# The low parts of down's coefficients on GpSimd instead of VectorE, between its gathers

## The chip, the cores and the metric

The kernel runs on one core of one Trainium2 chip. The metric is the device time of one launch in microseconds (us), the median of several runs. Three runs of the kernel before took 1741.0, 1741.33 and 1743.81 us, so the median is 1741.33 us. The data are those of one decoder layer: 256 tokens, 2048 channels, 16384 experts.

## What is computed

One layer with a convolution part, a gated short convolution and, behind them, a mixture of rank-one experts ("PEER"). What matters here is the last step of the experts:

```python
def peer_block(x_tok, w_q, sub_keys, peer_u, peer_v):
    ...
    act = jax.nn.gelu(jnp.einsum('td,thkd->thk', x_tok, u_sel), approximate=False)
    coef = act * g.astype(act.dtype)
    v_sel = peer_v[experts]
    return jnp.einsum('thk,thkd->td', coef, v_sel)
```

Each token chooses 8 x 16 = 128 of the 16384 experts. The kernel computes the activations of all experts for all tokens (stage "up") and multiplies all of them, zero where an expert wasn't chosen, with all rows of peer_v (stage "down"). An exception: for the second half of the tokens (block 1) and the first half of the output columns, each token's 128 chosen rows are gathered and added one by one.

## The kernel before

**Split products.** A product in full fp32 is made of three products in the fast format fp32r: an operand is split into a high part (a copy by ScalarE, rounded to fp32r) and a low part (the original less the high part). TensorE multiplies high by high, high by low and low by high. For each unit of weights of 128 x 1024 fp32, the stream is: SyncE's queue loads it into a buffer (`raw` or `raw_late`, 7 of them in down), ScalarE makes `w_hi` (L643, in `hi`), VectorE makes `w_lo` (L863, in `lo`), TensorE uses both. There are four pairs `w_hi`, `w_lo`, so ScalarE may be at most three units ahead of TensorE (`HLEAD`, `LEAD`). A buffer `raw` is reloaded when the low part has been made.

**Down.** 256 units, in 32 groups of four tiles of hidden activations. A group's coefficients, 128 x 1024 fp32, are a slice of `hid`. ScalarE copies it to `c_hi` (L796, `coef_hi`), VectorE subtracts to make `c_lo` (L1323, `coef_lo`). Both parts are the stationary operands of TensorE's matmuls (L1640 to L1642, 512 columns each); the even groups up to 27 hold one unit that goes unsplit in fp32 (L1651, 4 matmul records). Groups 0 to 27 use two sets `c0` and `c1` in turns (`coef_slot`). ScalarE makes `c_hi` of group g + 1 when TensorE has begun group g (the table `coef_at`), and VectorE makes `c_lo` of it at the same place of its own list, so that it is ready almost a group ahead. Each group of 8 units has 72 matmuls (fewer with an unsplit unit): units of 6, 6, 12, 12, 6, 6, 12 and 12, as each of the four column chunks is made for one or two blocks of tokens (`ORDER`, `blocks_of`). TensorE's `group` waits for the count `clo_done` before a group's first matmul.

**The picks.** For the gathered part, GpSimd's queue issues two kinds of indirect DMAs, one pair after the other (`gather_rows`, L597: 128 rows of 4 KB, one per token; `gather_acts`, L603: 128 single coefficients). VectorE adds row k times its coefficient to an accumulator in PSUM (`pick`, L1342, 128 of them). There are four row buffers (three `rows`, and `row_late`), so row k is gathered when pick k - 4 is done (`picked_done`). The numbers of the units at which VectorE makes each pick are fixed (`pick_unit`), one in 1.77 units. `acts_issued` lets the first eight turns issue two coefficient gathers per row gather and the later ones one; there are none behind row 115. Gathered coefficients are used in eights, a good way behind.

**The order** on each engine is written out by hand, and each engine works through its own list in order. VectorE's loop over the units of down, in words: the low part three units ahead, the coefficients' low part if one is due here, the picks that are due here, the next unit. GpSimd's list in down is a row gather with its coefficient gather(s), again and again.

## Time and profile before

| | us |
|---|---|
| median of 3 runs | 1741.33 |
| the profiled execution, its time | 1742.71 |
| the profiled execution, its span | 1740.7 |
| TensorE busy | 1703.1 (98%) |
| VectorE busy | 1459.6 (84%) |
| ScalarE busy | 849.1 (49%) |
| GpSimd busy | 530.5 (30%) |

The span is what the trace covers; the run's own time has 2.0 us around it. TensorE's granted clock was 1.00 (its upper level, 2.4 GHz) from end to end but for the first and last few us. Down begins near 1180 us and ends near 1726 us. A row of the timeline gives start, duration and, in brackets, how long the engine had been idle and what ended that; "issue" is time in which it waited for nothing that the profile shows. PEld is TensorE's weight load. The busy time of matmuls is modelled, and their rows overlap.

### The profile page before, as it was taken

Reading aid. Unit: us, or ns where it says so; the run is one execution under the profiler, and the core shown is the slowest. Engines: PE = TensorE matmul, PEld = TensorE weight load, DVE = VectorE, ACT = ScalarE, POOL = GpSimd, SP = SyncE. Lnnn points to the kernel's source line nnn. Section 1 sums busy time; section 2 is a strip of 40 time slices with the busy share of each in tenths; the row PEclk is TensorE's granted clock in tenths of the full one; section 3 lists DMA queues with packets and bytes.
Section 4 is the critical chain, followed back from the end, with each engine's and each line's share of the span. In section 5 each row is a group of like instructions: output and inputs, shape, how many; then the busy total and the mean of one; then the engine's idle time right before and its main releaser. Section 6 shows DMA issues by size and latency. Waiting matters only on the chain.

```text
span 1740.7 us, 27889 instructions
## 1 busy us (share of the span) xinstructions
PE 1703.1 (98%) x10124; PEld 1495.6 (86%) x10124; DVE 1459.6 (84%) x2095; ACT 849.1 (49%) x1071; POOL 530.5 (30%) x342
## 2 busy tenths in 40 slices
PE   9999999899999999999999999999999999999997
PEld 9999987799999888888888888887777777777876
DVE  7999997678968788888888888666898889899997
ACT  5544436344544444544444444445455554555544
POOL 0000000287881000000000000004786767687731
PEclk9999999999999999999999999999999999999999
DMA  7787787777777777777777777898999999999994
GB/s 278 261 276 260 238 254 254 282 237 233 248 254 247 241 240 243 245 237 242 237 242 238 239 242 246 285 355 310 344 390 396 398 399 394 397 372 399 401 407 141
DMA packets 173757, 504.73 MB, mean 290 GB/s; under 512 B 19424, under 2 KB 35936, under 8 KB 172640
## 3 DMA queue, kind: packets, MB, share of 16 engines
q1 hardware_dynamic: 134000, 427.08, 71.0%
q0 software_dynamic: 22528, 67.19, 10.1%
q10 hardware_dynamic: 17136, 9.35, 1.8%
q8 instruction: 41, 0.67, 0.2%
q14 instruction: 52, 0.43, 0.1%
HBM read 490.98 MB, written 79.69 MB: 328 GB/s over the span
## 4 chain that ended last, share of the span: by engine, by line
PE 81%; DMA 6%; DVE 5%; issue 4%; POOL 2%; ACT 1%; DVEq 0%; SPq 0%; POOLq 0%; ACTq 0%
PE psum L1461 22%; PE psum L1462 12%; PE psum L1446 8%; PE psum L1444 8%; PE psum L1445 8%; PE psum L1640 5%; PE psum L1642 5%; PE psum L1641 5%; DMA raw<-in_v_w_dram 4%; DVE w_lo L863 2%; PE psum L1606 2%; POOL sp_coef L603 2%; PE psum L1464 1%; DMA rows<-v_rows,sp_idx 1%; PE psum L1510 1%
## 5 line engine op out<-in xcount | busy, mean ns | idle before, releaser
L643 ACT ACTIVATE w_hi<-raw 128x1024 fp32r<-128x1024 f32 x540 | 571.6, 1060 | 645.9 <-PE psum L1464 180.7
L863 DVE TENSOR_TENSOR w_lo<-raw,w_hi 128x1024 fp32r<-128x1024 f32 x472 | 574.5, 1224 | 139.7 <-ACT w_hi L643 137.0
L1461 PE MATMUL psum<-xt,w_hi 128*128 128x512 f32 x1650 | 583.1, 393 | 0.1
L1462 PE MATMUL psum<-xt,w_lo 128*128 128x256 f32 x1760 | 476.9, 281 | 0.0
L1461 PEld LDWEIGHTS psum<-xt,w_hi 128*128 128x128 f32 x1650 | 309.5, 188 | 63.2 <-issue 0.4
L597 POOL DMA_INDIRECT rows<-v_rows,sp_idx x96 | 135.1, 1407 | 720.7 <-issue 672.7
L1462 PEld LDWEIGHTS psum<-xt,w_lo 128*128 128x128 f32 x1760 | 331.9, 189 | 9.4
L1444 PE MATMUL psum<-xt,w_hi 128*128 128x256 f32 x1184 | 333.8, 282 | 3.1 <-issue 1.9
L1446 PE MATMUL psum<-xt,w_lo 128*128 128x256 f32 x1184 | 332.2, 281 | 0.0
L1445 PE MATMUL psum<-xt,w_hi 128*128 128x256 f32 x1184 | 330.5, 279 | 0.0
L1640 PE MATMUL psum<-w_hi,c_hi 128*128 128x512 f32 x726 | 290.1, 400 | 16.2 <-DVE w_lo L863 13.9
L1642 PE MATMUL psum<-w_hi,c_lo 128*128 128x512 f32 x726 | 282.8, 390 | 0.0
L1641 PE MATMUL psum<-w_lo,c_hi 128*128 128x512 f32 x726 | 282.8, 390 | 0.0
L586 POOL TENSOR_TENSOR w_lo<-raw,w_hi 128x1024 fp32r<-128x1024 f32 x68 | 164.6, 2427 | 363.4 <-ACT w_hi L643 363.3
L1444 PEld LDWEIGHTS psum<-xt,w_hi 128*128 128x128 f32 x1184 | 223.4, 189 | 3.6 <-issue 3.6
L1445 PEld LDWEIGHTS psum<-xt,w_hi 128*128 128x128 f32 x1184 | 223.5, 189 | 0.0
L1446 PEld LDWEIGHTS psum<-xt,w_lo 128*128 128x128 f32 x1184 | 223.1, 188 | 0.0
L603 POOL DMA_INDIRECT sp_coef<-hid_spill,sp_idx x128 | 176.8, 1381 | 53.9 <-issue 44.2
L1640 PEld LDWEIGHTS psum<-w_hi,c_hi 128*128 128x128 f32 x726 | 136.2, 188 | 57.6 <-DVE w_lo L863 23.9
L1641 PEld LDWEIGHTS psum<-w_lo,c_hi 128*128 128x128 f32 x726 | 136.3, 188 | 29.8 <-issue 2.6
L1642 PEld LDWEIGHTS psum<-w_hi,c_lo 128*128 128x128 f32 x726 | 136.3, 188 | 28.9
L643 ACT ACTIVATE w_hi<-raw_late 128x1024 fp32r<-128x1024 f32 x99 | 105.0, 1060 | 110.6 <-PE psum L1642 74.0
(175 smaller groups left out, 1695.2 us busy)
## 6 DMA issues: line engine op xcount, KB each, us to landing
raw<-in_u_w_dram SPq DMA_DIRECT2D x256, 512.0 KB
raw<-in_v_w_dram SPq DMA_DIRECT2D x148, 512.0 KB
v_rows<-in_v_w_dram SPq DMA_DIRECT2D x128, 512.0 KB, 5.2
raw_late<-in_v_w_dram SPq DMA_DIRECT2D x108, 512.0 KB
raw<-in_w_in_dram SPq DMA_DIRECT2D x80, 512.0 KB
raw<-in_w_out_dram SPq DMA_DIRECT2D x32, 512.0 KB
raw<-in_w_q_dram SPq DMA_DIRECT2D x32, 512.0 KB
hid_spill<-hid ACTq DMA_DIRECT2D x7, 1024.0 KB, 14.3
```

The costliest lines, as they stand in the source:

```text
L586: nc.gpsimd.tensor_tensor(w_lo[s][:, :], raw[:, s, :], w_hi[s][:, :].bitcast(f32), ALU.subtract).then_inc(lo_done[s], SPLIT)
L603: nc.gpsimd.indirect_dma_start(sp_coef[:, k:k + 1], None, hid_dram, bass.IndirectOffsetOnAxis(sp_idx[:, 0, k:k + 1], 0)).then_inc(act_in[k ...
L643: nc.scalar.activation(parts_of(slot_u)[0][:, :], raw_of(slot_u), ACT.Copy)\
L863: tt(lo_w[:, :], raw_of(slot_u), hi_w[:, :].bitcast(f32), ALU.subtract).then_inc(lo_done[slot_u % SPLIT], lo_step(u))
L1444: mm(dst, hi_w[:, sl], xt_hi[:, kk, :], start=st, stop=False)
L1445: mm(dst, hi_w[:, sl], xt_lo[:, kk, :], start=False, stop=False)
L1446: i = mm(dst, lo_w[:, sl], xt_hi[:, kk, :], start=False, stop=en)
L1461: mm(both, hi_w[:, sl], x_both, start=st, stop=False)
L1462: i = mm(both[:, 0:T], lo_w[:, sl], xt_hi[:, kk, :], start=False, stop=False)
L1640: mm(v_bank(j, b), c1, w1, start=st, stop=False)
L1641: mm(v_bank(j, b), c1, w2, start=False, stop=False)
L1642: i = mm(v_bank(j, b), c2, w1, start=False, stop=en)
```

## The change

GpSimd makes `c_lo` of groups 3 to 27 (`CLO_POOL = (3, G_LAST)`), 25 of 32, with the same operation on the same operands. VectorE keeps groups 0 to 2 and 28 to 31. The operation stands in GpSimd's list behind the row gather `gathered_before(g)` and its coefficient gather: that is the gather which waits for the last pick ahead of the place where VectorE made this `c_lo`. A new count, `clo_pool`, is raised by it; `wait_clo` makes each of those who waited for `clo_done` wait for the right one: TensorE at the start of each group, SyncE's queue at units 64 and 112 of down (for groups 4 and 8), ScalarE for groups 14 and 22.

```diff
+CLO_POOL = (3, G_LAST)
...
+def on_pool(g):
+
+    return CLO_POOL[0] <= g < CLO_POOL[1]
...
+def gathered_before(g):
+
+    at = U_DOWN + 2 * NCH * (g - 1) + 1
+    return len([k for k in range(PICKS) if pick_unit(k) < at]) + ROWS - 1
...
+        def wait_clo(engine, g):
+
+            a, b = CLO_POOL
+            if g >= a:
+                engine.wait_ge(clo_pool, min(g, b - 1) - a + 1)
+            if not on_pool(g):
+                engine.wait_ge(clo_done, g + 1 - (b - a if g >= b else 0))
...
+            def coef_lo_pool(g):
+                hi_c, lo_c = c_sets[coef_slot(g)]
+                pool.wait_ge(chi_done, g + 1)
+                nc.gpsimd.tensor_tensor(lo_c[:, :, :], hid[:, GROUP * g:GROUP * (g + 1), :],
+                                        hi_c[:, :, :].bitcast(f32), ALU.subtract).then_inc(clo_pool, 1)
...
             for k in range(ROWS, PICKS):
                 gather_rows(k)
                 gather_acts(acts_issued(k - 1), acts_issued(k))
+                for g in range(*CLO_POOL):
+                    if gathered_before(g) == k:
+                        coef_lo_pool(g)
...
             def coef_lo(g):
+                if on_pool(g):
+                    return
                 hi_c, lo_c = c_sets[coef_slot(g)]
...
             def group(g, slot, first=False):
-                pe.wait_ge(clo_done, g + 1)
+                wait_clo(pe, g)
```

Lines move by 21 to 32: the row gather is L618 in the changed kernel, the coefficient gather L624, the new operation L631, VectorE's `w_lo` L893, its `c_lo` L1355, a pick L1374, TensorE's three matmuls L1672 to L1674.

GpSimd's list where it reaches group 3 (`rows2` is gather 6, `row_late` gather 7, `rows0` gather 8). Before:

```order
L597 DMA rows2<-v_rows,sp_idx 128x1024 [waits picked_done]
L603 DMA sp_coef<-hid_spill,sp_idx 128x1 x2
L597 DMA row_late<-v_rows,sp_idx 128x1024 [waits picked_done]
L603 DMA sp_coef<-hid_spill,sp_idx 128x1 x2
L597 DMA rows0<-v_rows,sp_idx 128x1024 [waits picked_done]
```

Now:

```order
L618 DMA rows2<-v_rows,sp_idx 128x1024 [waits picked_done]
L624 DMA sp_coef<-hid_spill,sp_idx 128x1 x2
L631 TENSOR_TENSOR c1_lo<-hid,c1_hi 128x1024 [waits chi_done]
L618 DMA row_late<-v_rows,sp_idx 128x1024 [waits picked_done]
L624 DMA sp_coef<-hid_spill,sp_idx 128x1 x2
L618 DMA rows0<-v_rows,sp_idx 128x1024 [waits picked_done]
```

The low part of group 3 now stands between gather 6 with its two coefficient gathers and gather 7; every gather behind it is queued behind it and behind its wait for `c_hi`.

VectorE's list at the same group (the picks of rows 1 and 2 with the `w_lo` between them). Before:

```order
L1342 SCALAR_TENSOR_TENSOR psum<-rows1,sp_coef,psum 128x1024 [waits picked_done,rows_in1,coef_done]
L863 TENSOR_TENSOR w_lo2<-raw,w_hi2 128x1024 [waits hi_done]
L863 TENSOR_TENSOR w_lo3<-raw,w_hi3 128x1024 [waits hi_done]
L1323 TENSOR_TENSOR c1_lo<-hid,c1_hi 128x1024 [waits chi_done]
L1342 SCALAR_TENSOR_TENSOR psum<-rows2,sp_coef,psum 128x1024 [waits picked_done,rows_in2,coef_done]
```

Now:

```order
L1374 SCALAR_TENSOR_TENSOR psum<-rows1,sp_coef,psum 128x1024 [waits picked_done,rows_in1,coef_done]
L893 TENSOR_TENSOR w_lo2<-raw,w_hi2 128x1024 [waits hi_done]
L893 TENSOR_TENSOR w_lo3<-raw,w_hi3 128x1024 [waits hi_done]
L1374 SCALAR_TENSOR_TENSOR psum<-rows2,sp_coef,psum 128x1024 [waits picked_done,rows_in2,coef_done]
L893 TENSOR_TENSOR w_lo0<-raw,w_hi0 128x1024 [waits hi_done]
```

The pick of row 2 now follows the second `w_lo` directly, and with it everything behind moves up by one place.

## Rows read from the trace of the kernel before

**Rows 1.** the page, section 1: busy us (share of the span) by engine.
```profile
PE 1703.1 (98%) x10124; PEld 1495.6 (86%) x10124; DVE 1459.6 (84%) x2095; ACT 849.1 (49%) x1071; POOL 530.5 (30%) x342
```

**Rows 2.** windows of three stretches of down: busy us (x instructions) by engine, clock, DMA.
```profile
1210.00:1300.00 90.00, 84.47 (x356) 65.94 (x355) 76.97 (x69) 43.77 (x42) 70.95 (x55) 1.00 0.96 358
1300.00:1500.00 200.00, 193.59 (x820) 152.58 (x819) 174.97 (x156) 102.42 (x98) 139.84 (x105) 1.00 1.03 397
1500.00:1645.00 145.00, 142.20 (x607) 113.17 (x606) 136.49 (x122) 78.02 (x76) 115.50 (x78) 1.00 1.01 390
```

**Rows 3.** waits of PEld, 1210 to 1645: us in total, times, longest.
```profile
PEld psum L1640 <- DVE w_lo L863: 21.2, 20, 2.3
```

**Rows 4.** lines of VectorE, 1300 to 1500.
```profile
L863 DVE TENSOR_TENSOR w_lo<-raw,w_hi 128x1024 fp32r<-128x1024 f32 x49 | 59.5, 1226 | 2.7 <-ACT w_hi L643 2.6
L863 DVE TENSOR_TENSOR w_lo<-raw_late,w_hi 128x1024 fp32r<-128x1024 f32 x37 | 44.8, 1222 | 1.8 <-ACT w_hi L643 1.6
L1323 DVE TENSOR_TENSOR c_lo<-hid,c_hi 128x1024 fp32r<-128x1024 f32 x12 | 14.7, 1226 | 20.1 <-ACT c_hi L796 19.9 <-issue 0.3
```

**Rows 5.** one line, L1323, the low parts: ns min/median/max, first and last start.
```profile
L1323 DVE TENSOR_TENSOR c_lo<-hid,c_hi x32: 1217/1226/1229, 1159.5 to 1650.7; 128x1024 fp32r<-128x1024 f32 x32
```

**Rows 6.** lines of GpSimd, 1210 to 1300.
```profile
L603 POOL DMA_INDIRECT sp_coef<-hid_spill,sp_idx x30 | 36.0, 1200 | 10.4 <-issue 10.4
L597 POOL DMA_INDIRECT rows<-v_rows,sp_idx x19 | 26.8, 1411 | 7.0 <-issue 5.9 <-DVE psum L1342 1.1
L597 POOL DMA_INDIRECT row_late<-v_rows,sp_idx x6 | 8.5, 1416 | 1.8 <-issue 1.5 <-DVE psum L1342 0.3
```

**Rows 7.** lines of GpSimd, 1300 to 1500.
```profile
L603 POOL DMA_INDIRECT sp_coef<-hid_spill,sp_idx x53 | 68.9, 1300 | 16.1 <-issue 16.1
L597 POOL DMA_INDIRECT rows<-v_rows,sp_idx x39 | 54.6, 1399 | 34.6 <-DVE psum L1342 25.6 <-issue 9.0
L597 POOL DMA_INDIRECT row_late<-v_rows,sp_idx x13 | 17.2, 1323 | 8.2 <-DVE psum L1342 5.2 <-issue 3.0
```

**Rows 8.** lines of GpSimd, 1500 to 1645.
```profile
L603 POOL DMA_INDIRECT sp_coef<-hid_spill,sp_idx x38 | 61.6, 1622 | 11.6 <-issue 11.6
L597 POOL DMA_INDIRECT rows<-v_rows,sp_idx x30 | 41.0, 1367 | 16.4 <-DVE psum L1342 9.1 <-issue 7.2
L597 POOL DMA_INDIRECT row_late<-v_rows,sp_idx x10 | 14.5, 1452 | 3.0 <-issue 2.7 <-DVE psum L1342 0.3
```

**Rows 9.** one line, L586: GpSimd's own subtraction, ns min/median/max, first and last start.
```profile
L586 POOL TENSOR_TENSOR w_lo<-raw,w_hi x68: 2365/2403/2871, 324.9 to 527.8; 128x1024 fp32r<-128x1024 f32 x68
```

**Rows 10.** timeline, a gather behind two w_lo: GpSimd, then VectorE.
```profile
1506.92 3.17 POOL L597 DMA_INDIRECT row_late<-v_rows,sp_idx  x1 [0.30 <-issue]
1506.91 2.36 DVE L863 TENSOR_TENSOR w_lo<-raw,w_hi 128x1024 fp32r<-128x1024 f32 x2
```

**Rows 11.** one line, L1273 (both inputs in SBUF) and L1180 (one in PSUM).
```profile
L1273 DVE TENSOR_TENSOR oh<-oh,gate_p x32: 691/692/2775, 525.6 to 1076.9; 128x1024 bf16<-128x1024 bf16 x32
L1180 DVE TENSOR_TENSOR psum<-tab_f,psum x8: 1219/1219/1228, 452.0 to 475.5; 128x1024 f32<-128x1024 f32 x8
```

**Rows 12.** timeline of that L1273: VectorE, and GpSimd beside it.
```profile
525.56 2.77 DVE L1273 TENSOR_TENSOR oh<-oh,gate_p 128x1024 bf16<-128x1024 bf16 x1
524.92 5.69 POOL L586 TENSOR_TENSOR w_lo<-raw,w_hi 128x1024 fp32r<-128x1024 f32 x2 [0.26 <-ACT w_hi L643]
```

**Rows 13.** timeline at the start of group 4: GpSimd, then TensorE.
```profile
1247.56 0.95 POOL L603 DMA_INDIRECT sp_coef<-hid_spill,sp_idx  x1 [0.30 <-issue]
1248.81 1.41 POOL L597 DMA_INDIRECT row_late<-v_rows,sp_idx  x1 [0.30 <-issue]
1249.55 0.47 PE L1640 MATMUL psum<-w_hi,c_hi 128*128 128x512 f32 x1 [0.86 <-issue]
```

**Rows 14.** timeline ahead of group 7: GpSimd, then TensorE in group 6.
```profile
1297.94 0.95 POOL L597 DMA_INDIRECT rows<-v_rows,sp_idx  x1 [0.31 <-issue]
1295.49 1.88 PE L1651 MATMUL psum<-raw,hid 128*128 128x512 f32 x4
```

More of the change, by code:

```diff
@@ L430, in build @@
         clo_late = sem("clo_late")
+        clo_pool = sem("clo_pool")
         ln2_in = sem("ln2_in")
@@ L540, in _ @@
                     sp.wait_ge(hid_out, 16 * DUMPS)
-                    sp.wait_ge(clo_done, 5)
+                    wait_clo(sp, 4)
                 if n == LN2_AT:
-                    sp.wait_ge(clo_done, 9)
+                    wait_clo(sp, 8)
                 i, at = divmod(n - X1_BACK_AT, PIECE_STEP)
@@ L638, in hi @@
                 if isinstance(u, int) and u >= U_END - SPLIT:
-                    act.wait_ge(clo_done, 23)
+                    wait_clo(act, 22)
                     act.wait_ge(hid_out, 16 * DUMPS)
@@ L789, in coef_hi @@
                 elif g > G_LAST:
-                    act.wait_ge(clo_done, 15)
+                    wait_clo(act, 14)
                     act.wait_ge(hid_out, 16 * DUMPS)
@@ L1675, in _ @@
                     if j == ORDER[0] and g == G_LAST:
-                        pe.wait_ge(clo_done, G_LAST + 1)
+                        wait_clo(pe, G_LAST)
                     elif j == ORDER[0]:
```

## The prediction

> **What bounds the kernel now.** I read the page first, then the windows of down, then who waits for whom there, and last GpSimd's rows one by one, since it is the engine that gets work.
>
> GpSimd is busy for 30% of the span [rows 1], which looks like room. The share is an average over stages, though, and the 25 operations all go into the stretch from 1210 to 1645 us. There [rows 2] TensorE is busy for 84.5 of 90, 193.6 of 200 and 142.2 of 145 us, VectorE for 77.0, 175.0 and 136.5, GpSimd for 71.0, 139.8 and 115.5, and the DMA engines are full (share 0.96, 1.03, 1.01; 358, 397 and 390 GB/s). So TensorE is nearly bound by its own matmuls, DMA is at its ceiling in the middle, and no engine of the three has much left. What the change can give back is small: TensorE's weight loads wait 21.2 us for `w_lo`, in 20 waits, about one per group [rows 3].
>
> How full GpSimd really is, its rows by stretch show. Its DMA instructions are followed by about 0.3 us each that the profile calls "issue"; only the waits for a pick ("DVE psum L1342") are true idle time.
> - 1210 to 1300 [rows 6]: 71.3 us busy, 17.8 issue, 1.4 idle.
> - 1300 to 1500 [rows 7]: 140.7 busy, 28.1 issue, 30.8 idle.
> - 1500 to 1645 [rows 8]: 117.1 busy, 21.5 issue, 9.4 idle.
>
> **What goes.** VectorE loses 25 subtractions of 1.226 us [rows 5]. In 1300 to 1500, 12 of them are busy for 14.7 us, and VectorE stands idle for 19.9 us before them, waiting for `c_hi` [rows 4]. That wait was partly free, since the next `w_lo` needs its own `w_hi`. The gain is that `w_lo` and picks no longer queue behind it.
>
> **What comes: the price of one.** GpSimd has run this very form 68 times in the q stage: 2403 ns median [rows 9]. To that come 0.3 us of issue. Then the two engines hold each other up, and the rows show it both ways. A gather that started 0.01 us behind two `w_lo` took 3.17 us [rows 10], where one undisturbed takes 0.94 to 0.95 [rows 13, 14]. In the other direction, VectorE's L1273, with both inputs in SBUF, has a median of 0.69 us, but took 2.77 the one time when it started inside a GpSimd subtraction [rows 11, 12]; L1180, with one input in PSUM, ran in the same stage and never took over 1.228 [rows 11]. `w_lo` has both inputs in SBUF, so it will stand still for what is left of GpSimd's 2.4 us; a pick, with its accumulator in PSUM, will not. How long the new operation is itself held up by a `w_lo`, no row shows, so I bound it: nothing, if VectorE happens to be at a pick, and 2.2 us (3.17 less 0.95) behind two `w_lo`. The nearest rows are GpSimd's gathers in the same stretches: 1.34 us on average in the middle (140.7/105) against 0.95, so 0.4 us. I take 2.4 + 0.3 + 0.4 = **3.1 us** per group.
>
> VectorE becomes less of a hindrance by what it loses: `c_lo` is 14.7 of its 119.0 us of operations with two SBUF inputs (14.7 + 59.5 + 44.8, [rows 4]), 12%. The time above 0.95 per gather is 71.3 - 55 x 0.95 = 19 us in the first stretch, 41 in the second, 43 in the third [rows 6 to 8]; 12% of these gives GpSimd 2.3, 4.9 and 5.2 us back.
>
> On this the Trainium skill says something else: SBUF — State Buffer (§ Who interferes with whom) has a VectorE tensor_tensor with two SBUF inputs contend only with a GpSimd operation that reads SBUF, while descriptor generation needs the write side. By that alone the gathers' 0.4 us would not be VectorE's doing, nothing would come back, and the sum below would be 12.4 us higher. The rows tie the two together, so I go by them.
>
> **The sum, by stretch.** The groups count by the 25 places of `c_lo` in VectorE's rows, which are a group apart: 5 (groups 3 to 7), 12 (8 to 19), 8 (20 to 27).
>
> *1210 to 1300.* GpSimd has no idle time, and it is late: group 4's operation comes behind gather 10, whose place ends at 1248.8, while TensorE begins group 4 at 1249.55 [rows 13]. In the kernel before, VectorE had made it long before that. With 3.1 us for group 3 and as much for itself it ends near 1254.7. So **TensorE waits for `c_lo`**, which it never did. At the end of the stretch the lag is 5 x 3.1 - 1.4 - 2.3 = 11.8 us. Group 7's is due where gather 25 starts, at 1297.94, so it ends at 1297.94 + 11.8 - 0.3 = 1309.4. TensorE would begin group 7 at 1303.0: the unsplit unit of group 6 from 1295.49, 1.88 us long [rows 14], then 24 matmuls at 142.2/607 = 0.234 us [rows 2]. That is **+6.4 us**.
>
> *1300 to 1500.* 12 x 3.1 = 37.2, less 30.8 of idle time and 4.9: **+1.5**. Here the idle time nearly pays.
>
> *1500 to 1645.* 8 x 3.1 = 24.8, less 9.4 and 5.2: **+10.2**.
>
> Each us of GpSimd's lag counts in full once TensorE waits for it. While it waits, though, weights come in and are split, so that some of the 21.2 us of waits for `w_lo` [rows 3] go. None of them is the low bound and all the high one; most lie in the middle stretch, where GpSimd decides least, so I credit a quarter, **-5**.
>
> VectorE's own balance I take as nothing: per group it is freed of 1.2 us and a wait of up to 1.7 (19.9/12), and may be held up for up to 2.4. SyncE's and ScalarE's moved waits cost nothing: they ask for groups 4, 8, 14 and 22 at times when the groups that far on are running. Behind 1645 the gathers need no coefficient gathers beside them, and nothing is added.
>
> Sum: 6.4 + 1.5 + 10.2 - 5 = **+13.1 us** on the profiled execution's own 1742.7, so 1755.8. The median of the runs lies 1.4 below that execution: **1754**.
>
> **The rivals.**
>
> *A. As forecast: GpSimd is the bound.* Its own ends: no hold-up (-0.4 x 25 = -10) gives 1744; a hold-up of 0.8 (+10), no relief (+12) and no credit (+5) give 1781. Chance 0.56.
>
> *B. Faster: GpSimd's new work is hidden.* It decides at GpSimd's price per group: below 1.8 us in the last stretch ((9.4 + 5.2)/8) and with the first stretch's lag kept below the lead at group 4, nothing is late. That could be if the instructions to issue gathers overlap the subtraction, which rows of this engine can't exclude. TensorE then gets back its waits for `w_lo`, at group starts, where `c_lo` stood in front. The ceiling is DMA's: 358 x 90 + 397 x 200 + 390 x 145 = 168,200 in GB/s x us, which at the middle's 397 takes 423.7 instead of 435 us, -11.3 us: 1730. For it speaks that the wait for `c_hi` is real; against it the 1.4 us of idle time at the start. Chance 0.20.
>
> *C. No difference.* The mutual hold-up is smaller than thought and the gain eats the lag: 1741, within 3.5. Chance 0.12.
>
> *D. Only the hold-up of VectorE counts.* GpSimd keeps up, but each of its 25 operations stops a `w_lo` for up to 2.4 us where 1.2 were freed, 25 x 1.2 = 30 us of VectorE's time, which has 8.5 us left in the last stretch and 25 in the middle; the stretches' spare time covers all but 1 us of that on the whole, and none of the 30 if each falls where a `w_lo` is due. It is nearer to the lower end, since VectorE is three units ahead; I take 5 us: 1746. Chance 0.12. The same page of the Trainium skill (same section) calls the shared port an exclusive lock for the whole instruction; with that, [rows 12] agree.
>
> That the change doesn't do what it says I leave out: the order of GpSimd and VectorE shows 25 operations gone from one and put on the other.
>
> **The numbers.** A change within 0.2% (3.5 us) is about what a measurement of this kernel can't tell from none. Slower is A and D, 0.68; same C, 0.12; faster B, 0.20. The range reaches from just inside B, 1732, to near A's upper end, 1778; A alone would be 1744 to 1781.
>
> **What would show it.** TensorE's rows should have a wait for GpSimd's L631 that wasn't there, longest at group 4 (3 to 6 us), again from group 20 on, 10 to 20 us in all. L631 should last 2.4 us at least and up to 4.6, a `w_lo` beside it up to 3.6. GpSimd's waits for picks should fall from 41.6 us to under 15, and its last stretch be full. I am wrong if TensorE never waits for L631 and the waits for `w_lo` shrink (B), or if these waits grow instead (D).

## The result and the profile after

| | us |
|---|---|
| after, median of 6 runs | 1754.44 (1750.69 to 1759.76) |
| before, median of 6 runs beside them | 1742.51 (1740.13 to 1745.2) |
| ratio, 95% interval | 1.0072, 1.0058 to 1.0087 |
| profiled execution after, its time and span | 1754.97, 1753.2 |

The change makes the kernel slower by 0.72%, 12.5 us (10 to 15). The forecast was 1754 and slower.

The page of the changed kernel, section 1 (busy us and share by engine), against [rows 1]:

```profile
PE 1707.6 (97%) x10124; PEld 1497.1 (85%) x10124; DVE 1473.3 (84%) x2070; ACT 848.5 (48%) x1071; POOL 578.2 (33%) x367
```

VectorE lost 25 operations of 1.226 us and is nevertheless busy for 13.7 us more. GpSimd gained 47.7 us for 25 operations of some 2.4 (61 us). Windows of the three stretches after (busy us of PE, PEld, DVE, ACT, POOL with instructions, then clock, DMA share, GB/s), against [rows 2]:

```profile
1210.00:1300.00 90.00, 82.19 (x336) 63.12 (x335) 75.36 (x61) 41.19 (x41) 72.28 (x55) 0.98 0.94 341
1300.00:1500.00 200.00, 192.78 (x812) 152.54 (x811) 181.23 (x146) 100.53 (x97) 168.96 (x117) 0.99 1.02 390
1500.00:1645.00 145.00, 137.97 (x580) 108.73 (x579) 133.60 (x108) 76.60 (x74) 119.30 (x80) 0.99 1.00 385
```

TensorE lost 2.3, 0.8 and 4.2 us of busy time, its clock left 1.00 in every stretch, and DMA moved 17, 7 and 5 GB/s less. Where the time went within down is best read from the unsplit units, which both kernels have at the same places of the program. The line of these matmuls before, in four short windows (min/median/max of the durations, then the starts of the unit's first and last matmul record; they are the units of groups 2, 8, 20 and 26):

```profile
L1651 PE MATMUL psum<-raw,hid x4: 590/592/592, 1225.0 to 1226.3; 128*128 128x512 f32 x4
L1651 PE MATMUL psum<-raw,hid x4: 591/592/592, 1329.5 to 1330.8; 128*128 128x512 f32 x4
L1651 PE MATMUL psum<-raw,hid x4: 590/592/593, 1540.3 to 1541.5; 128*128 128x512 f32 x4
L1651 PE MATMUL psum<-raw_late,hid x4: 590/592/592, 1639.8 to 1641.1; 128*128 128x512 f32 x4
```

and after:

```profile
L1683 PE MATMUL psum<-raw,hid x4: 590/592/592, 1223.8 to 1225.1; 128*128 128x512 f32 x4
L1683 PE MATMUL psum<-raw,hid x4: 590/592/592, 1334.6 to 1335.9; 128*128 128x512 f32 x4
L1683 PE MATMUL psum<-raw,hid x4: 590/592/593, 1545.1 to 1546.4; 128*128 128x512 f32 x4
L1683 PE MATMUL psum<-raw_late,hid x4: 590/592/592, 1652.1 to 1653.4; 128*128 128x512 f32 x4
```

From group 2 (after is 1.2 us ahead there) to group 8 the change costs 6.3 us, from 8 to 20 it gives 0.3 back, from 20 to 26 it costs 7.5. The waits of the changed kernel between 1210 and 1657 us (us in total, times, longest):

```profile
PEld psum L1672 <- DVE w_lo L893: 28.4, 29, 2.5
PEld psum L1672 <- POOL c_lo L631: 3.6, 2, 3.2
PE psum L1672 <- DVE w_lo L893: 19.2, 20, 2.8
DVE w_lo L893 <- ACT w_hi L673: 15.4, 16, 2.2
DVE psum L1374 <- DMA rows<-v_rows,sp_idx: 15.0, 8, 4.4
DVE psum L1374 <- issue: 9.4, 10, 2.4
DVE psum L1374 <- DMA row_late<-v_rows,sp_idx: 3.2, 4, 1.5
POOL rows L618 <- DVE psum L1374: 8.6, 18, 0.9
POOL row_late L618 <- DVE psum L1374: 2.3, 4, 0.9
```

Before, in the same window:

```profile
PEld psum L1640 <- DVE w_lo L863: 21.2, 20, 2.3
PE psum L1640 <- DVE w_lo L863: 12.4, 14, 1.9
DVE c_lo L1323 <- ACT c_hi L796: 26.2, 19, 2.8
```

TensorE's matmuls wait 19.2 us for `w_lo` instead of 12.4, and 2.8 us for the new operation besides. All idle time of the matmuls in the window is 22.1 us instead of 14.8, 7.3 more; with the three falls of the clock shown below (some 5 us) that is the whole 12.3 us by which the profiled execution is longer. The chain of work that ended last, by engine (section 4 of the page, shares of the whole span), before and after:

```profile
PE 81%; DMA 6%; DVE 5%; issue 4%; POOL 2%; ACT 1%; DVEq 0%; SPq 0%; POOLq 0%; ACTq 0%
PE 77%; POOL 9%; DMA 5%; DVE 4%; issue 4%; ACT 1%; DVEq 0%; SPq 0%; POOLq 0%; ACTq 0%
```

GpSimd's share of it rises from 2% to 9%. VectorE no longer waits for `c_hi` (26.2 us), but for `w_hi` 15.4 instead of 4.7 us, and its picks for gathered rows 27.6 (15.0 + 9.4 + 3.2) instead of 11.0 (5.7 for the rows and 5.3 of "issue"). The "issue" part, 9.4 and 5.3, is counted in here although the profile names nothing for it; without it the waits are 18.2 and 5.7.

GpSimd waits for picks 12.2 (10.9 here and 1.3 for the first pick) instead of 46.6 us ([rows 6 to 8] had 41.6 of it up to 1645): its slack has gone. The new operation's line, who waits for it in all, and `w_lo` from `raw` (ns min/median/max):

```profile
L631 POOL TENSOR_TENSOR c_lo<-hid,c_hi x25: 2362/2412/2761, 1228.7 to 1652.8; 128x1024 fp32r<-128x1024 f32 x25
  PEld psum L1672: 6.8, 3
L893 DVE TENSOR_TENSOR w_lo<-raw,w_hi x108: 1210/1218/4111, 1215.5 to 1656.2; 128x1024 fp32r<-128x1024 f32 x108
```

L631 was held up by 0.35 us at most: 2.36 to 2.76 us, as in the q stage [rows 9]. `w_lo`, which never took over 1.273 us before in this window, takes up to 4.1. Its 187 instructions here are busy for 267.9 us (162.0 and 105.9, the line groups), some 40 more than 187 x 1.22. Counted one by one, 24 of them take over 1.3 us, together 42.3 us over 1.22 each; this count is the "hold" in what follows. GpSimd's own groups (us busy, mean ns):

```profile
L624 POOL DMA_INDIRECT sp_coef<-hid_spill,sp_idx x119 | 134.2, 1127 | 38.2 <-issue 38.2
L618 POOL DMA_INDIRECT rows<-v_rows,sp_idx x85 | 133.0, 1564 | 28.9 <-issue 18.9 <-DVE psum L1374 8.6 <-DVE psum L1371 1.3
L631 POOL TENSOR_TENSOR c_lo<-hid,c_hi 128x1024 fp32r<-128x1024 f32 x25 | 61.0, 2441 | 0.5
```

Before, the mean coefficient gather was 1378 ns and the mean row gather 1395. So one kind of gather is relieved and the other made longer. The longer ones have a place: each of the 25 row gathers right behind an L631 took 1.76 to 2.02 us, 1.78 on average; the other 89 row gathers in this stretch took 1.48. The same 25 rows took 1.36 in the kernel before. The head of group 4, TensorE first:

```profile
1249.44 0.39 PE L1674 MATMUL psum<-w_hi,c_lo 128*128 128x512 f32 x1
1252.65 0.47 PE L1672 MATMUL psum<-w_hi,c_hi 128*128 128x512 f32 x1 [2.82 <-DVE w_lo L893]
...
1253.19 0.61 PE L1674 MATMUL psum<-w_hi,c_lo 128*128 128x512 f32 x1
...
1256.58 0.41 PE L1673 MATMUL psum<-w_lo,c_hi 128*128 128x512 f32 x1
```

and beside it GpSimd's two rows and VectorE's one (two `w_lo` merged):

```profile
1249.04 2.37 POOL L631 TENSOR_TENSOR c_lo<-hid,c_hi 128x1024 fp32r<-128x1024 f32 x1
1251.57 1.76 POOL L618 DMA_INDIRECT row_late<-v_rows,sp_idx  x1 [0.16 <-issue]
1248.83 4.81 DVE L893 TENSOR_TENSOR w_lo<-raw,w_hi 128x1024 fp32r<-128x1024 f32 x2
```

L631 starts at 1249.04, 0.8 us ahead of the moment when TensorE has nothing left of group 3 (1249.83). It ends at 1251.41. The first of the two `w_lo`, begun 0.21 us before it, stands still for it: the two take 4.81 us instead of 2.4. So at 1251.41 `c_lo` is there, but `w_lo` isn't, and TensorE goes on at 1252.65, 2.82 us late. (1.6 us of these until `c_lo` was there, 1.2 more until `w_lo` was.) The row gather behind L631 takes 1.76 us. The matmuls are then 0.43 us apart instead of 0.23 for eight of them, from 1253.19 to 1256.58: TensorE's clock is at its lower level (1.2 GHz), which costs 8 x 0.2 = 1.6 us more. The other such place is the head of group 26: GpSimd, VectorE, TensorE.

```profile
1633.99 3.16 POOL L618 DMA_INDIRECT rows<-v_rows,sp_idx  x1 [0.30 <-issue]
...
1638.41 2.36 POOL L631 TENSOR_TENSOR c_lo<-hid,c_hi 128x1024 fp32r<-128x1024 f32 x1
1633.97 2.36 DVE L893 TENSOR_TENSOR w_lo<-raw,w_hi 128x1024 fp32r<-128x1024 f32 x2
1638.58 3.29 DVE L893 TENSOR_TENSOR w_lo<-raw,w_hi 128x1024 fp32r<-128x1024 f32 x1
1640.83 0.50 PE L1672 MATMUL psum<-w_hi,c_hi 128*128 128x512 f32 x1 [2.77 <-POOL c_lo L631]
```

Here the gather ahead of the operation started with two `w_lo` and took 3.16 us, as in [rows 10]. That is 2.2 us over an undisturbed gather and the likely reason why L631 is late. TensorE stands for 2.77 us until it ends, and its clock is lower again from 1.5 us later on.

### The profile page after: what moved, and what is told of

It reads as the page before. It is cut to its first block, busy times and chain, and to the rows that moved or that the text cites. A ratio compares the mean times of both kernels' runs of the same rounds, so it can differ in the third digit from the quotient of the medians.

```text
span 1753.2 us, 27889 instructions
## 1 busy us (share of the span) xinstructions
PE 1707.6 (97%) x10124; PEld 1497.1 (85%) x10124; DVE 1473.3 (84%) x2070; ACT 848.5 (48%) x1071; POOL 578.2 (33%) x367
## 2 busy tenths in 40 slices
DMA packets 173758, 504.73 MB, mean 288 GB/s; under 512 B 19424, under 2 KB 35936, under 8 KB 172640
## 4 chain that ended last, share of the span: by engine, by line
PE 77%; POOL 9%; DMA 5%; DVE 4%; issue 4%; ACT 1%; DVEq 0%; SPq 0%; POOLq 0%; ACTq 0%
PE psum L1493 21%; PE psum L1494 12%; PE psum L1476 8%; PE psum L1477 8%; PE psum L1478 8%; PE psum L1672 4%; PE psum L1674 4%; PE psum L1673 4%; POOL sp_coef L624 4%; POOL rows L618 3%; DMA rows<-v_rows,sp_idx 2%; PE psum L1638 2%; POOL c_lo L631 2%; PE psum L1496 1%; DMA raw_late<-in_v_w_dram 1%
## 5 line engine op out<-in xcount | busy, mean ns | idle before, releaser
L893 DVE TENSOR_TENSOR w_lo<-raw,w_hi 128x1024 fp32r<-128x1024 f32 x472 | 605.6, 1290 | 141.2 <-ACT w_hi L673 138.3
L618 POOL DMA_INDIRECT rows<-v_rows,sp_idx x96 | 149.0, 1552 | 690.9 <-PE psum L1496 650.2
L1672 PE MATMUL psum<-w_hi,c_hi 128*128 128x512 f32 x726 | 292.7, 403 | 23.6 <-DVE w_lo L893 20.7
L1674 PE MATMUL psum<-w_hi,c_lo 128*128 128x512 f32 x726 | 284.7, 392 | 0.0
L1672 PEld LDWEIGHTS psum<-w_hi,c_hi 128*128 128x128 f32 x726 | 137.3, 189 | 67.5 <-DVE w_lo L893 31.4
L624 POOL DMA_INDIRECT sp_coef<-hid_spill,sp_idx x128 | 146.8, 1147 | 54.3 <-issue 44.9
L1674 PEld LDWEIGHTS psum<-w_hi,c_lo 128*128 128x128 f32 x726 | 137.4, 189 | 29.5
```

Of the source, the lines that this page charges most:

```text
L618: nc.gpsimd.indirect_dma_start(rows[k % ROWS][:, :], None, v_rows, bass.IndirectOffsetOnAxis(sp_idx[:, 1, k:k + 1], 0)).then_inc(rows_in[k ...
L624: nc.gpsimd.indirect_dma_start(sp_coef[:, k:k + 1], None, hid_dram, bass.IndirectOffsetOnAxis(sp_idx[:, 0, k:k + 1], 0)).then_inc(act_in[k ...
L893: tt(lo_w[:, :], raw_of(slot_u), hi_w[:, :].bitcast(f32), ALU.subtract).then_inc(lo_done[slot_u % SPLIT], lo_step(u))
L1672: mm(v_bank(j, b), c1, w1, start=st, stop=False)
L1674: i = mm(v_bank(j, b), c2, w1, start=False, stop=en)
```

## The experiments

The theory: GpSimd's own time has run out (A of the prediction), with a price of 3.1 us each. Its rival: VectorE's held `w_lo` is the cost (D). The third question was whether there is a gain to be had at all from taking `c_lo` away (B). In all runs the times are medians; the ratio is to the kernel before on the same chip.

### No operation at all: `none`

```diff
-                engine.wait_ge(clo_pool, min(g, b - 1) - a + 1)
+            if on_pool(g):
+                engine.wait_ge(chi_done, g + 1)
...
-                    if gathered_before(g) == k:
-                        coef_lo_pool(g)
+                    pass
```

The low parts of groups 3 to 27 are left out (what lies in the buffer is used).

> The changed kernel without the 25 subtractions, on GpSimd or anywhere: the low parts of groups 3 to 27 aren't made, TensorE reads what lies in their buffers and waits for the high parts alone. This is what VectorE's relief is worth by itself, with nothing in its place. Theory (the operation on GpSimd costs more than VectorE's relief gives): 6 to 11 us under before, about 1733, since DMA is full in the middle. Rival (the relief gives nothing since DMA bounds down anyway): within 3 us of before.

1739.03 us, ratio 0.9986 (0.9974 to 0.9998). All that taking `c_lo` off VectorE can give is some 2.4 us, and 4.5 at most by the interval. The 6 to 11 us expected were wrong, and the rival, within 3 us since DMA bounds down anyway, is what came. TensorE still waits 18.9 us for `w_lo` (19 waits) in the window, since VectorE now waits 49.6 us for `w_hi`: it runs ahead into ScalarE. And ScalarE has to wait for its weights to arrive: 124.7 us (74.6 and 50.1 for the two kinds of `raw`), against 76.6 before and 40.6 in the changed kernel.

```profile
ACT w_hi L672 <- DMA raw<-in_v_w_dram: 74.6, 67, 3.2
```

So what limits `none` is in good part the weights' transfers, and rival B's ceiling of 11 us doesn't exist in this form.

### GpSimd's time without the hold: `memset`

```diff
-                nc.gpsimd.tensor_tensor(lo_c[:, :, :], hid[:, GROUP * g:GROUP * (g + 1), :],
-                                        hi_c[:, :, :].bitcast(f32), ALU.subtract).then_inc(clo_pool, 1)
+                n = 2 * (g - CLO_POOL[0])
+                nc.gpsimd.memset(lo_c[:, :, :].bitcast(f32), 0.0).then_inc(fill, 1)
+                pool.wait_ge(fill, n + 1)
+                nc.gpsimd.memset(lo_c[:, :, :].bitcast(f32), 0.0).then_inc(fill, 1)
+                pool.wait_ge(fill, n + 2)
+                nc.gpsimd.memset(lo_c[:, 0:1, :].bitcast(f32), 0.0).then_inc(clo_pool, 1)
```

The low parts of these groups are zero. GpSimd is taken for about as long, at the same place, but reads no SBUF.

> The changed kernel with the subtraction on GpSimd replaced by three memsets of the same destination, some 2.4 us together, which read no SBUF; the low parts are zeros, their products are left out of the output. GpSimd is as long away from its gathers. Theory 1 (GpSimd's capacity: gathers and rows come late): as slow as after, 1752 to 1757, and GpSimd's waits for picks stay small. Theory 2 (the subtraction holds up w_lo on VectorE, and that is what costs): near the kernel without the operation, 1733 to 1740, with no w_lo over 1.3 us. Half and half would be near 1745.

1741.38 us, ratio 1.0003 (0.9988 to 1.0019). Its `w_lo` (those into `raw_late`; the others go up to 1.274 us):

```profile
L898 DVE TENSOR_TENSOR w_lo<-raw_late,w_hi x82: 1210/1219/1296, 1210.0 to 1650.2; 128x1024 fp32r<-128x1024 f32 x82
```

The three fills take 0.974 + 0.955 + 0.313 = 2.24 us, 56 us in all, against 61 for L631, and no `w_lo` is longer than 1.296 us beside them. The cost over `none` is 2.4 us in the medians (3 by the ratios). TensorE did wait for `c_lo` once, 2.5 us; its clock fell once, 30 us later. So **56 us more of GpSimd's time are nearly covered**: by its waits for picks (24.4 us are left) and by shorter gathers (1259 and 1255 ns on average, instead of 1378 and 1395).

But the load isn't quite that of L631. The row gather right behind the fills takes 1.17 us on average, and that behind L631 1.78. Operation and gather together are 2.44 + 1.78 = 4.22 us there, and 2.24 + 1.17 = 3.41 here: 0.8 us less, 20 in 25 groups.

By its own expectation the time speaks for the other theory: 1741.38 is far from the 1752 to 1757 of GpSimd's capacity, and near the upper end of what was expected if the hold is the cost. The load that is 20 us lighter is an explanation found afterwards. What this run shows is that GpSimd's slack reaches for the fills, and that the missing 13 us hang on what the subtraction does beyond taking 2.24 us of GpSimd's time: the hold, the longer gather behind it, or both.

### The hold without the load: `b_nc` and `a_nc`

```diff
-            gather_acts(0, acts_issued(ROWS - 1))
+            gather_acts(0, PICKS_IN)
...
-                gather_acts(acts_issued(k - 1), acts_issued(k))
...
-                if k % PICKS_IN == 0:
-                    pick_coefs(k // PICKS_IN)
-                dve.wait_ge(coef_done, k // PICKS_IN + 1)
+                if k == 0:
+                    pick_coefs(0)
+                dve.wait_ge(coef_done, 1)
...
-                    i = stt(picked[:, :], rows[k % ROWS][:, :], sp_coef[:, k:k + 1], picked[:, :], ALU.mult, ALU.add)
+                    i = stt(picked[:, :], rows[k % ROWS][:, :], sp_coef[:, k % PICKS_IN:k % PICKS_IN + 1], picked[:, :], ALU.mult, ALU.add)
```

The same edit on the kernel before (`b_nc`) and on the changed one (`a_nc`): 8 coefficient gathers instead of 128, so all picks use the first eight coefficients, over and over. GpSimd gets back some 190 us of idle time in the window (its waits for picks are 235 us in `b_nc`, 46.6 before).

> The kernel before with 8 coefficient gathers instead of 128; each pick uses one of the first eight coefficients again, so the gathered part of the output is wrong and its time right. GpSimd loses 120 of its 256 DMA instructions in down. As reference for the next. Theory 1: GpSimd's load matters, 1734 to 1740. Theory 2: hardly, 1738 to 1743.

> The changed kernel with the same 8 coefficient gathers, so that GpSimd has some 200 us of room for its 25 subtractions. Theory 1 (capacity): no cost over b_nc, or a gain of up to 4 us. Theory 2 (w_lo held up): still 8 to 14 us over b_nc.

1727.68 (0.9927, 0.9901 to 0.9953) and 1727.61 us (0.9923, 0.9897 to 0.9949). With an idle GpSimd the change costs nothing: the medians of four runs each are 0.1 us apart, and the intervals of both are some 4 us to either side. TensorE's wait for `w_lo` in `b_nc`:

```profile
PEld psum L1639 <- DVE w_lo L862: 7.9, 11, 1.1
```

and in `a_nc`, with its `w_lo` and VectorE's wait for rows:

```profile
PEld psum L1671 <- DVE w_lo L892: 11.0, 16, 1.1
L892 DVE TENSOR_TENSOR w_lo<-raw_late,w_hi x85: 1209/1217/3239, 1210.2 to 1649.8; 128x1024 fp32r<-128x1024 f32 x85
DVE psum L1373 <- DMA rows<-v_rows,sp_idx: 0.9, 1, 0.9
```

L631 holds `w_lo` here too (up to 3.2 us; 20 of 201 instructions over 1.3 us, 21.5 us of hold), but rows are there in time (0.9 us of waits against 18.2 after), and VectorE makes up for it. The hold is half of what it is in the changed kernel (42.3 us), so the test is of this much: **21.5 us of held `w_lo` cost nothing where GpSimd has time.** And 13 us of the kernel before come from its coefficient gathers, more than expected. Most of that is likely GpSimd's time: VectorE loses only 15 products of 0.16 us with them, and the DMA engines 0.08 of 504.73 MB (though 3841 of 173757 packets).

### Only one stretch: `head`, `mid`, `tail`

```diff
-CLO_POOL = (3, G_LAST)
+CLO_POOL = (3, 8)
```

The others have `(8, 20)` and `(20, G_LAST)`: together they are the changed kernel, cut where the prediction cut it.

> Only the five groups 3 to 7 are made by GpSimd, all others by VectorE. Prediction by stretch: +6.4 us in 1210 to 1300, of which the middle's slack may give some back. If costs lie where the starts of the unsplit units of the changed kernel place them (+5.2 us up to group 8), 1744 to 1748, and TensorE still waits for L631 at groups 4 and 7. If the hold-up of VectorE is the cost wherever it falls and is paid back by nothing: 5/25 of 12 us, 1744. If the first stretch's delay is only a loan that the middle pays back: within 2 us of before.

> The changed kernel with only groups 8 to 19 on GpSimd, 12 of 25, in the stretch where GpSimd had 31 us of idle time. Theory 1 (capacity) as in the prediction: 12 operations cost about what the idle time pays, 1740 to 1744. Theory 2 (w_lo held up): each operation costs the same wherever it is, so 12/25 of the 12 us: 1746 to 1750.

> Only the eight groups 20 to 27 are made by GpSimd. Prediction by stretch: +10.2 us in 1500 to 1645. By the starts of the changed kernel's unsplit units (+7.4 us there), 1747 to 1750. If the cost goes with the number of operations alone: 8/25 of 12 us, +3.8, 1745. With the twelve of groups 8 to 19 at +2 the three parts would add up to the whole 12 only if head and tail bring 10 between them; if they bring clearly less, the cost is one of the load being on in all stretches together.

| | groups | us | before | ratio, 95% | difference, us | by the prediction, ahead of the credit |
|---|---|---|---|---|---|---|
| `head` | 3 to 7 | 1748.7 | 1742.47 | 1.0029 (1.0015 to 1.0044) | +5.1 | +6.4 |
| `mid` | 8 to 19 | 1743.15 | 1740.99 | 1.0011 (0.9994 to 1.0027) | +1.9 | +1.5 |
| `tail` | 20 to 27 | 1749.37 | 1742.47 | 1.0039 (1.0023 to 1.0055) | +6.8 | +10.2 |

The differences are the ratio times the kernel before. They add up to 13.8 us, and the whole change costs 12.5: within the intervals, of some 2.5 us to either side of each, the cost of a stretch is its own, and the next pays nothing back. It doesn't go with the number of operations: 12 of them in the middle cost less than 5 at the start (`mid` by itself can't be told from nothing). Nor does it go with the hold, which is 7.0 us in `head` (4 `w_lo`), 12.6 in `mid` (9) and 12.5 in `tail` (6). TensorE's wait for L631 in `head` (window as above; those for `w_lo` are 22.9 us):

```profile
PEld psum L1672 <- POOL c_lo L631: 5.4, 2, 2.9
```

In `tail` it is one wait of 3.4 us, at the head of group 26 again, beside 24.7 for `w_lo`; its profiled execution is the slowest of its twelve. In `head` the two waits stand for 4.5 us in the matmuls' rows, and the clock fell too (0.98 in the first stretch); the fall at 1254.6 is worth 1.7. Together they cover the 5.1 that it costs. The waits are at the heads of groups 3 and 4, and not at 4 and 7 as expected. `mid` has no wait for L631 at all. It is the stretch in which GpSimd had 30.8 us of idle time [rows 7]; the others had 1.4 and 9.4. At 3.1 us an operation GpSimd lacks 14.1 us in `head`, 6.4 in `mid` and 15.4 in `tail`, and the costs, 5.1, 1.9 and 6.8, are 0.36, 0.30 and 0.44 of these. **The costs go with what GpSimd lacks**: that is A's order. D's fits less well, but `mid` and `tail` alone wouldn't rule it out, since VectorE too had more idle time in the middle (25 us, against 8.5 in the last stretch [rows 2]); it is `head`, with 13 us of VectorE's idle time, 7.0 of hold and 5.1 of cost, that speaks against it. `head`'s median is just above the 1744 to 1748 expected; `mid` and `tail` lie in their ranges.

### The operation one gather later, and in halves: `later` and `halves`

```diff
-    return len([k for k in range(PICKS) if pick_unit(k) < at]) + ROWS - 1
+    return len([k for k in range(PICKS) if pick_unit(k) < at]) + ROWS - 1 + 1
```

> The changed kernel with each GpSimd operation one row gather later. The operation's length and its hold on a w_lo stay. If TensorE's waits for c_lo are part of the cost they grow: 3 waits of 6.8 us become 8 or more of 25 us and the time goes to 1760 or above. If the cost is the hold-up of VectorE, the time stays at 1751 to 1757.

1755.32 us, ratio 1.007 (1.0048 to 1.0093). (Its profiled execution is the fastest of its six, 1747.29.) The waits in it:

```profile
PEld psum L1672 <- DVE w_lo L893: 12.8, 19, 1.6
PEld psum L1672 <- POOL c_lo L631: 11.4, 5, 4.7
```

TensorE's waits for `c_lo` have grown from 3.6 us (6.8 by L631's own line) to 11.4 and those for `w_lo` have fallen from 28.4 to 12.8. The expectation that these would add up, to 1760 or more, was wrong; 1755 is where it has the time if VectorE's hold is the cost. In this execution one wait takes the other's place. (It is 8 us faster than the changed kernel's profiled one, though, so the waits of the two can't be set against each other closely.) In the medians the time is the same.

`halves` makes the operation in two of 128 x 512, the second behind the next gather:

```diff
-                    if gathered_before(g) == k:
-                        coef_lo_pool(g)
+                    for part in range(2):
+                        if gathered_before(g) + part == k:
+                            coef_lo_pool(g, part)
```

> The changed kernel with each subtraction cut in two of 128 x 512, the second one gather later. Theory 2 (hold-up of w_lo): the longest hold is halved from 2.4 to about 1.3 us, which fits within the lead of VectorE: 1744 to 1750. Theory 1 (capacity): the same work plus one more issue, 1754 or more.

1752.5 us, ratio 1.0067 (1.0042 to 1.0091). The halves last 1348 ns each, 2.7 us the pair. The longest `w_lo` is 2.98 us and the hold 31.5 us in all instead of 42.3; TensorE waits 15.5 us for `c_lo` (6 waits) and 13.2 for `w_lo`. A quarter less of hold, and again the same time within the interval: between the two expectations, nearer to that of GpSimd's capacity.

### VectorE keeps it: `late2`, `late4`, `twice`

```diff
-                if u in coef_at:
-                    coef_lo(coef_at[u])
+                if u - 2 in coef_at:
+                    coef_lo(coef_at[u - 2])
```

This is the kernel before, with its `c_lo` two units later in VectorE's list (four in `late4`). `twice` is `late2` with every `c_lo` of groups 3 to 27 made two times in a row, 30.6 us more work for VectorE:

```diff
+                if on_pool(g):
+                    tt(lo_c[:, :, :], hid[:, mine, :], hi_c[:, :, :].bitcast(f32), ALU.subtract).then_inc(clo_first, 1)
+                    dve.wait_ge(clo_first, g - 2)
```

> The kernel before, c_lo still on VectorE for all groups, but two units later in VectorE's list, so that neither w_lo nor picks stand behind its wait for c_hi (25 us in before). If the gain the change was after lies in that wait, this takes it without GpSimd: 1734 to 1740. If DMA bounds it or the wait was free, 1741 to 1743. A c_lo that comes too late for TensorE would show as a wait for it and make it slower.

> The kernel before with VectorE's c_lo four units later instead of at once, and nothing on GpSimd. Two units later took its wait for c_hi away and gave 0.9986. If that wait was all there was to gain, 1737 to 1740 again. If c_lo then comes too near TensorE's group start, TensorE waits for it (L1323) at some groups: 1741 to 1746.

> Late2 (c_lo on VectorE, two units later) with each c_lo of groups 3 to 27 made twice, one after the other, on VectorE; GpSimd has nothing of it. VectorE is taken up for 2.45 us per group at once, as by a hold of 2.4 us. Theory 2, if a hold is no more than VectorE's time: 10 to 14 us over late2, near 1750. If it comes out at 1742 or less, time of VectorE alone isn't what after pays, and the moment of the hold or the lateness of rows behind it matters.

`late2`: 1737.98 us, ratio 0.9986 (0.9973 to 0.9998). `late4`: 1741.9, 0.9995 (0.9979 to 1.0011). `twice`: 1746.03, 1.0021 (1.0004 to 1.0038). In `late2` the wait for `c_hi` is gone, but it reappears one step on, as a wait for `w_hi` (4.7 us before):

```profile
DVE w_lo L863 <- ACT w_hi L643: 31.4, 42, 1.7
```

So the wait for `c_hi`, which looked like 26 us of VectorE's time, is worth 2.4 us at most, as in `none`: ScalarE itself waits for weights (127.9 us instead of 76.6) and for TensorE (86.7). `late4` has neither a wait for `c_hi` nor one of TensorE's for `c_lo`, and gains nothing that can be told, so even the 2.4 us aren't sure. `late2` computes everything, and is 15 us faster than the changed kernel (1.0072 less 0.9986); against the kernel before it lies within what can't be told from nothing. `twice` gives the price of VectorE's time on the other side: 30.6 us of it cost 6 us (1.0021 less 0.9986), about a fifth. That is half of the 10 to 14 expected if a hold is no more than VectorE's time, and above the 1742 that would have made that time count for nothing.

## Why the prediction was right, and where it wasn't

**The size and the sign.** Forecast +13.1 on the profiled execution; measured 12.5 in the medians and 12.3 in the profiled ones (1754.97 - 1742.71). The split by stretch held in the main: +6.4, +1.5 and +10.2 ahead of the credit, against +6.3, -0.3 and +7.5 in the unsplit units, and +5.1, +1.9 and +6.8 by `head`, `mid` and `tail`. The step that carried this was to count GpSimd's idle time by stretch instead of reading 30% off the page. That the amounts agree this well is in part luck. The +6.4 stood for a wait at the head of group 7, with the new operation ending at 1309.4. It ended at 1304.55 and TensorE reached group 7 only near 1306.6, so there was no such wait: the stretch lost its time at group 4, through the clock and in waits for `w_lo`. And several terms were off in directions that cancel, as follows.

**The mechanism.** That GpSimd's time is needed for the cost is what the runs show. `a_nc`, with GpSimd unloaded, costs nothing with 21.5 us of hold. `head` costs 5.1 us with two waits for L631 and 7.0 us of hold; `mid`, where GpSimd had idle time, costs 1.9 with 12.6. But the way from GpSimd to TensorE is mostly another than the prediction's. It had TensorE wait for `c_lo`; these waits are 4.4 us of the 12.3 (2.8 at group 26 and 1.6 at group 4). The rest is the clock and longer waits for `w_lo`, which the prediction had shrink. The likely path is that a row gather comes late, the pick behind it waits (27.6 us for rows, 11.0 before), and so does the next `w_lo`; no run isolates it. What D adds isn't settled. `memset` has neither the hold nor the longer gather behind the operation, and both of these lie between its 1741 and the 1754 of the changed kernel. No run has one without the other on a loaded GpSimd. A part of the 12 us may be VectorE's: by `twice`, 30.6 us of its time cost 6, and the hold is 42.3 us where 31.9 of `c_lo` went.

**The head of group 4.** TensorE stopped there, as the prediction had it, for 2.8 us (forecast 3 to 6). But L631 began at 1249.04 and not near 1251.6: the lag of 3.1 us for group 3 wasn't there. Only 1.6 us of the stop were for `c_lo`, the rest for a held `w_lo`. The second such place is the head of group 26; a third wait, at group 3, is 0.36 us. In all the waits are 6.8 us in 3, by the line of L631 above, against 10 to 20 forecast. `later` shows that this amount decides little, since a wait for `c_lo` stands where one for `w_lo` would.

**The price, 3.1 us.** The 2.4 held (2.44 on average). The hold-up of 0.4 had the right size in the wrong place: it was looked for at the operation, which is hardly ever held; it falls on the row gather behind it, with 0.42 (1.78 us against 1.36 for the same rows before). And the 0.3 of issue is not added: 0.02 us ahead of L631 and 0.16 behind stand where 0.30 stood before, 0.1 less. 2.44 + 0.42 - 0.1 = 2.8.

**The relief, 12.4 us.** On the two pages GpSimd's busy time rose by 47.7 us (530.5 to 578.2), for 61.0 of new work and 25 x 0.42 = 10.4 of longer gathers behind it. So 23.7 came back, nearly twice the forecast. It is mostly the coefficient gathers: 0.25 us less each in the window (119 x 0.25 = 30), while the row gathers took 0.17 and 0.08 more (85 x 0.17 + 29 x 0.08 = 17, with the 10.4 in it). But the reason wasn't the prediction's, that VectorE has 12% fewer such subtractions. `none` has them gone and nothing in their place, and its mean coefficient gather fell from 1378 to 1244 ns; `late2` has every one of them still on VectorE, and the fall is the same:

```profile
L603 POOL DMA_INDIRECT sp_coef<-hid_spill,sp_idx x120 | 149.6, 1247 | 41.8 <-issue 41.8
```

What counts is when a gather meets a subtraction. Of the kernel before's 239 gathers in the window, 56 ran beside one of VectorE's two-input subtractions (`w_lo`, `c_lo`) for less than 0.1 of their first 0.95 us, and all of these took 0.94 to 0.96 us; 115 ran beside them for 0.9 us or more and took 1.76 on average. In `late2` these are 48 and 95. Why their number changes stays open. The rule that the prediction weighed here (the Trainium skill, SBUF — State Buffer, § Who interferes with whom: descriptor generation needs the write side, a tensor_tensor takes only reads, which the section itself calls inferred) would give no such difference. Both kinds of gather also read their index, `sp_idx`, from SBUF, so they may fall under the section's rule for reads; no run here separates the two. The same section says that a GpSimd operation that only writes doesn't contend with such a subtraction: `memset` agrees, with its longest `w_lo` at 1.296 us.

**The credit, -5.** This step failed. The waits for `w_lo` didn't shrink by a quarter, but grew from 21.2 to 28.4 us, which the prediction had named as the sign of D. Another overestimate hid it, and that is luck: that each us of GpSimd's lag counts in full. By `head`, `mid` and `tail` the cost is 13.8 us where GpSimd lacks 35.9 ahead of the relief; the prediction, with relief, had 18.1.

**VectorE's balance, taken as nothing.** Freed: 31.9 us of `c_lo` (35.5 to 3.6) and its wait of 26.2. Taken back: 42 us of longer `w_lo`, 10.7 more for `w_hi`, 16.6 more for rows. That is 58 against 70, with terms several times as large as the whole forecast, and a balance that by `twice`'s fifth would be some 2 us.

**The clock** stood in no term. Its three falls cost about 5 us of the 12 in the profiled execution (below).

**Rivals.** B's ceiling came from DMA's rate; `none` shows that with `c_lo` gone altogether TensorE's waits for `w_lo` remain, so what it priced wasn't `c_lo`'s to give. D as the only cost is out: in `a_nc` 21.5 us of hold cost nothing, and `head` costs most per operation, with waits for L631 itself. D as a part of the cost isn't, as said above. C is out by the interval.

## What to carry to other kernels

Before work is moved to an engine that looks idle, count its idle time in the stretch where the work will lie: 12 operations in the middle cost 1.9 us, 5 at the start 5.1. Price the operation with the one behind it, which may be the one that is held. And test what the relieved engine gains by leaving the work out altogether: that run alone said that no more than some 2.4 us were to be had here. A forecast that comes out right is still to be checked term by term: here the time agreed while the wait that should have made it was a third of it.

## What the runs showed of the hardware

**A stop of 2 to 3 us can cost TensorE its clock.** In the changed kernel it went to its lower level three times in down, for 3.4 us each (the window's clock of 0.98 in 90 us and 0.99 in the others): near 1253.2, 1427.3 and 1642.3, each 0.5 to 1.5 us behind the end of an idle time, of 2.82, 2.07 and 2.77 us. The place of the second, where TensorE's idle time was one for `w_lo` alone:

```profile
1425.91 0.50 PE L1672 MATMUL psum<-w_hi,c_hi 128*128 128x512 f32 x1 [2.07 <-DVE w_lo L893]
...
1427.54 0.63 PE L1672 MATMUL psum<-w_hi,c_hi 128*128 128x512 f32 x1
1427.97 0.63 PE L1673 MATMUL psum<-w_lo,c_hi 128*128 128x512 f32 x1
```

Here, too, the matmuls go from 0.23 to 0.43 us apart. The kernel before, `mid`, `late4`, `b_nc` and `a_nc`, whose longest idle time of TensorE in this window is 0.7 to 1.9 us, kept 1.00 there. `none` (3.3), `late2` (3.9), `memset` (2.5), `twice` (3.1), `head` (2.5), `tail` (3.5), `later` (4.3) and `halves` (3.7) fell once or more. But the length of one stop doesn't decide it. In `memset` the stop of 2.52 us up to 1248.75 had no fall behind it, and that of 1.79 up to 1278.59 had one at once; in `head` 2.04 us up to 1234.48 had none:

```profile
1248.75 0.50 PE L1677 MATMUL psum<-w_hi,c_hi 128*128 128x512 f32 x1 [2.52 <-POOL c_lo L637]
1278.59 0.63 PE L1677 MATMUL psum<-w_hi,c_hi 128*128 128x512 f32 x1 [1.79 <-DVE w_lo L898]
```

A fall of 3.4 us at half the clock costs some 1.7, so a wait of 2.8 us with a fall behind it costs 4.5.

**GpSimd's subtraction goes ahead of a `w_lo` that began before it.** At 1249.04 it came 0.21 us behind the first `w_lo`, took 2.37 us, and the `w_lo` stood. So it was in six of the changed kernel's 25, with a `w_lo` that had begun 0.03 to 0.62 us earlier (these took 3.5 to 4.1 us). In five others the `w_lo` had begun 0.73 to 0.97 us earlier: it took its 1.22 to 1.26 us, and L631 2.55 to 2.76. The Trainium skill (SBUF — State Buffer, § SBUF: two separate sides) has whichever starts first get the shared pair for the whole instruction, VectorE's instructions with two SBUF inputs against a GpSimd operation that reads SBUF included; for this pair of subtractions the rows show GpSimd winning from second place.
